# Two of the four normalisations in halves of 512 tokens, and the last FFN product behind the barrier

## What is computed

```
h = rms_norm(x, norm1_w); proj = h @ w_in                      # first
h2 = rms_norm(x, norm2_w); ... x + (silu(gate) * up) @ w_ffn_down   # second
h = rms_norm_2(x, g_pre); proj = h @ w_in_2                    # third
x = x + rms_norm_2(merged @ w_out, g_post)                     # fourth
```

## Time and profile before

| | |
|---|---|
| time, median of 3 runs | 3429.97 us (3427.22 to 3436.2) |
| the profiled execution | 3430.34 us |
| its span, first to last instruction | 3428.4 us |
| TensorE busy | 3283.3 us, 96% of the span |
| VectorE, ScalarE, GpSimd busy | 1479.0, 1012.7, 1315.8 us |
| mean granted TensorE clock | 0.983 |

### The profile page before, as it was taken

The page is one execution under the profiler, slowest core; times in us unless marked ns, Lnnn a source line. Parts: engine busy times, 40 slices in busy tenths (PEclk is TensorE's granted clock), DMA queues, the critical chain, the costliest instruction groups (busy, mean ns, idle before and its releaser), DMA issues. The chain is left out here.

```text
span 3428.4 us, 51094 instructions
## 1 busy us (share of the span) xinstructions
PE 3283.3 (96%) x20680; PEld 2707.5 (79%) x20680; DVE 1479.0 (43%) x2368; ACT 1012.7 (30%) x1728; POOL 1315.8 (38%) x1102
## 2 busy tenths in 40 slices
PE   6999999999898999999999999999899999999999
PEld 5888888777787887887788888888688877777877
DVE  4333333263656555457633333333382144444343
ACT  3444444432443434301211111111222044432221
POOL 4222222252424242335434333344434355554543
PEclk9999999999999999999899999999899999999999
DMA  2100000103112011214111111111331111111122
GB/s 105 36 32 32 31 32 32 38 22 112 37 32 56 20 49 28 87 54 156 51 57 49 43 49 49 49 49 49 120 87 47 48 46 42 52 46 46 58 86 80
DMA packets 104198, 188.06 MB, mean 55 GB/s; under 512 B 32328, under 2 KB 64712, under 8 KB 101328
## 3 DMA queue, kind: packets, MB, share of 16 engines
q1 hardware_dynamic: 91536, 179.19, 16.0%
q10 hardware_dynamic: 12480, 6.29, 0.6%
HBM read 158.33 MB, written 27.12 MB: 54 GB/s over the span
## 5 line engine op out<-in xcount | busy, mean ns | idle before, releaser
L303 PE MATMUL DP<-XH,WH 128*128 128x512 f32 x2592 | 832.6, 402 | 18.3 <-POOL WL L251 18.3
L249 POOL CAST WH<-WRAW 128x1024 fp32r<-128x1024 f32 (+2 forms) x258 | 269.2, 1043 | 1484.2 <-issue 900.5
L303 PE MATMUL DP<-XL,WH 128*128 128x512 f32 x2592 | 804.7, 392 | 0.0
L303 PE MATMUL DP<-XH,WL 128*128 128x512 f32 x2592 | 803.5, 391 | 0.0
L251 POOL TENSOR_TENSOR WL<-WRAW,WH 128x1024 fp32r<-128x1024 f32 (+2 forms) x258 | 588.5, 2281 | 20.8
L303 PEld LDWEIGHTS DP<-XH,WL 128*128 128x128 f32 x2592 | 488.7, 189 | 105.6
L303 PEld LDWEIGHTS DP<-XL,WH 128*128 128x128 f32 x2592 | 488.8, 189 | 105.0
L303 PEld LDWEIGHTS DP<-XH,WH 128*128 128x128 f32 x2592 | 467.6, 189 | 120.0 <-issue 24.3
L870 DVE SCALAR_TENSOR_TENSOR SS<-B,RQ,SBI 128x256 f32<-128x256 f32 (+2 forms) x192 | 74.3, 428 | 314.8 <-PE B L569 314.8
L379 DVE TENSOR_TENSOR XR<-XR,B 128x1024 f32<-128x1024 f32 x88 | 106.6, 1220 | 90.7 <-PE B L359 88.4
L2320 DVE SCALAR_TENSOR_TENSOR TG<-DP,COL,TG 128x1023 f32<-128x1023 f32 x44 | 56.4, 1283 | 199.8 <-ACT TG L2308 197.0
(11 more groups left out here) (480 smaller groups left out, 5176.3 us busy)
## 6 DMA issues: line engine op xcount, KB each, us to landing
WRAW<-in_w_up SPq DMA_DIRECT2D x44, 512.0 KB, 3.5
WRAW<-in_w_attn SPq DMA_DIRECT2D x36, 512.0 KB, 3.5
WRAW<-in_w_down SPq DMA_DIRECT2D x22, 512.0 KB, 3.5
XR<-in_x SPq DMA_DIRECT2D x8, 1024.0 KB, 8.0
WRAW<-in_w_dn SPq DMA_DIRECT2D x16, 512.0 KB, 3.8
aa_dram<-AA ACTq DMA_DIRECT2D x12, 512.0 KB, 3.3
YY<-yy_dram SPq DMA_DIRECT2D x12, 512.0 KB, 4.1
WRAW<-in_w_lrux SPq DMA_DIRECT2D x10, 512.0 KB, 3.4
```

Of the source, the lines that this page charges most:

```text
L249: pool.tensor_copy(WH[b.slot][:, 0:b.kt, :], WRAW[b.slot][:, 0:b.kt, :]).then_inc(w_hi, 1)
L303: mm = pe.matmul(DP[b.slot][:, half * H:half * H + H], w[b.slot][:, k, :], x[:, k, half * H:half * H + H], start=one, stop=end)
```

## The change

The tokens of c1 and c3 are cut in two halves; every step of the normalisation is done for tokens 0 to 511 and for 512 to 1023 by operations of half the size, in an order written out by hand. The product that follows does all eight tiles of the first half, then the second (`product2_halves`), with `norm_sum` and `norm_turn` of the second half at tiles 4 and 6 of the first. XR is loaded in halves, the second halves behind the first two weight blocks. VectorE's chain `prep_dve` is cut: its first nine operations (`prep_angle`) stay at the front, the other 21 stand behind the whole normalisation. Their two stores move from SyncE's queue to ScalarE's, and ScalarE waits for them (pr_sm) in front of attention. In c3, block ffn1 7 is computed by halves behind the barrier (`product4_halves`), which moves up to the end of block 6; s5x 1 gets a third buffer and both s5x splits stand right behind the barrier. The load of the root's table (`norm_warm`) is a step of its own. The second and fourth normalisations keep their form; counters are renumbered throughout, which is left out here with the rewritten helpers `norm_*`, which take a token range.

```diff
+        self.buf = 2 if (name, it, pos) == ("s5x", 0, 1) and isinstance(it, int) else pos % 2
...
-        WRAW = [at(f"WRAW{i}", 128 + 4 * i, [P, 8, P]) for i in range(2)]
-        WH = [at(f"WH{i}", 136 + 4 * i, [P, 8, P], F32R) for i in range(2)]
-        WL = [at(f"WL{i}", 144 + 4 * i, [P, 8, P], F32R) for i in range(2)]
+        WRAW = [at(f"WRAW{i}", 128 + 4 * i if i < 2 else 112, [P, 8, P]) for i in range(3)]
+        WH = [at(f"WH{i}", 136 + 4 * i if i < 2 else 116, [P, 8, P], F32R) for i in range(3)]
+        WL = [at(f"WL{i}", 144 + 4 * i if i < 2 else 120, [P, 8, P], F32R) for i in range(3)]
...
+            if b.before() is not None and b.buf < 2:
...
+        def product4_halves(pe, b, group, hi, lo, before):
+
+            pe.wait_ge(w_split, b.n + 1)
+            pe.wait_ge(psum_free[b.slot], b.loads - 1)
+            for half in range(2):
+                t = slice(half * H, half * H + H)
+                for o in range(4):
+                    pe.wait_ge(part_read, group * 4 + (o + 1 if half else o // 2 - 1))
+                    for k in range(2):
+                        before(half, o, k)
+                        for w, x, one, end in ((WH, hi, k == 0, False), (WH, lo, False, False), (WL, hi, False, k == 1)):
+                            mm = pe.matmul(BANK[4 + o], w[b.slot][:, 2 * o + k, :], x[:, k, t], start=one, stop=end)
+                    if half and o == 3:
+                        mm.then_inc(mm_done, 1)
+                    elif half or o:
+                        mm.then_inc(part_ready, 1)
+
+        def add_half(dve, b, group, half, o, dst, m0):
+
+            if half and o == 3:
+                dve.wait_ge(mm_done, b.n + 1)
+            else:
+                dve.wait_ge(part_ready, (group + half) * 3 + (o + 1 if half else max(o, 1)))
+            x = dst[:, m0 + o, half * H:half * H + H]
+            dve.tensor_tensor(x, x, BANK[4 + o], ALU.add).then_inc(part_read, 1)
+
...
+        def product2_halves(pe, blocks, hi, lo, cs, within=None):
+
+            for b in blocks:
+                pe.wait_ge(w_split, b.n + 1)
+                pe.wait_ge(psum_free[b.slot], b.loads - 1)
+            for half, c in enumerate(cs):
+                t = slice(half * H, half * H + H)
+                steps = [(b, k) for k in range(KD if half == 0 else 4) for b in blocks]
+                if half:
+                    steps += [(b, k) for b in blocks for k in range(4, KD)]
+                for b, k in steps:
+                    if b is blocks[0]:
+                        if half == 0 and within:
+                            within(k)
+                        pe.wait_ge(xh_ready, c.nt + k + 1)
+                        pe.wait_ge(nt_used, c.nt + k + 1)
+                    for w, x, one, end in ((WH, hi, k == 0, False), (WH, lo, False, False), (WL, hi, False, k == KD - 1)):
+                        mm = pe.matmul(DP[b.slot][:, t], w[b.buf][:, k, :], x[:, k, t], start=one, stop=end)
+                    if half and k == KD - 1:
+                        mm.then_inc(mm_done, 1)
 
         def norm_tiles(c):
...
+            def second_norm(k):
+                if k == 4:
+                    norm_sum(pe, c1[1])
+                if k == 6:
+                    norm_turn(pe, c1[1])
+
+            product2_halves(pe, [att_block(0, pos) for pos in range(2)], XH, XL, c1, second_norm)
...
+        def ffn_last_pe(pe):
+            def before(half, o, k):
+                if (half, o, k) == (1, 2, 1):
+                    norm_sum(pe, c3[0])
+
+            product4_halves(pe, Block("ffn1", 0, 7), FT - 1, FH2, FL2, before)
+            norm_turn(pe, c3[0])
+
+        def ffn_last_dve(dve):
+            a, b = c3
+            block, group = Block("ffn1", 0, 7), FT - 1
+
+            def add(half, o):
+                add_half(dve, block, group, half, o, XR, 4)
+
+            def scale(k):
+                scale_one(dve, a, k, XR, "gpre")
+
+            add4(dve, Block("ffn1", 0, 6), FT - 2, XR, (2,))
+            norm_add(dve, c3_all, 1)
+            add4(dve, Block("ffn1", 0, 6), FT - 2, XR, (3,))
+            norm_add(dve, c3_all, 2)
+            norm_add(dve, c3_all, 3)
+            add(0, 0)
+            for o in range(1, 4):
+                add(0, o)
+                norm_add(dve, a, 3 + o)
+            dve.sem_inc(psum_free[block.slot], 1)
+            norm_add(dve, a, 7)
+            add(1, 0)
+            norm_inverse(dve, a)
+            add(1, 1)
+            scale(0)
+            scale(1)
+            add(1, 2)
+            add(1, 3)
+            norm_add(dve, b, 4)
+            for k in range(2, 5):
+                scale(k)
+                norm_add(dve, b, k + 3)
+            scale(5)
+            scale(6)
+            norm_inverse(dve, b)
+            scale(7)
+            norm_scale(dve, b, XR, "gpre")
+
+        def ffn_last_act(act):
+            a, b = c3
+            act.wait_ge(fl_ready, FT)
+            for k in range(4):
+                act.wait_ge(part_read, (FT - 2) * 4 + k + 1)
+                norm_square(act, c3_all, k, XR[:, k, :])
+            norm_warm(act)
+            for k in range(4, KD):
+                act.wait_ge(part_read, (FT - 1) * 4 + k - 3)
+                norm_square(act, a, k, XR[:, k, a.tok])
+            norm_sqrt(act, a)
+
+            def square(k):
+                act.wait_ge(part_read, FT * 4 + k - 3)
+                norm_square(act, b, k, XR[:, k, b.tok])
+
+            hi_one(act, a, 0)
+            hi_one(act, a, 1)
+            square(4)
+            square(5)
+            hi_one(act, a, 2)
+            square(6)
+            hi_one(act, a, 3)
+            square(7)
+            for k in range(4, 7):
+                hi_one(act, a, k)
+            norm_sqrt(act, b)
+            hi_one(act, a, 7)
+            norm_hi(act, b)
 
...
-            sp.wait_ge(pr_sm, 1)
-            sp.dma_start(r8_dram, SM[:, 8, :]).then_inc(pr_out, 16)
-            sp.dma_start(sk_dram, SM[:, 13:27, :].rearrange("p r t -> p (r t)")).then_inc(pr_out, 16)
...
-        def prep_dve(dve):
+        def prep_angle(dve):
...
+        def prep_dve(dve):
...
-                    sp.dma_start(XR[:, 2 * i:2 * i + 2, :], a["x"][:, 2 * i:2 * i + 2, :]).then_inc(mx_in[i], 16)
+                    sp.dma_start(XR[:, 2 * i:2 * i + 2, 0:H], a["x"][:, 2 * i:2 * i + 2, 0:H]).then_inc(mx_in[i], 16)
...
+                for k, n, landed in ((0, 2, mx_out), (2, 2, ks_out), (4, 4, w1_out)):
+                    sp.dma_start(XR[:, k:k + n, H:T], a["x"][:, k:k + n, H:T]).then_inc(landed, 16)
...
-                split(pool, Block("s5x", 0, 0))
-                pool.wait_ge(sq_used, c3.acc + 7)
-                split(pool, Block("s5x", 0, 1))
...
+                def square1(i, k):
+                    act.wait_ge((mx_out, ks_out, w1_out, w1_out)[k // 2] if i else mx_in[k // 2], 16)
+                    norm_square(act, c1[i], k, XR[:, k, c1[i].tok])
+
                 for k in range(KD):
-                    act.wait_ge(mx_in[k // 2], 16)
-                    norm_square(act, c1, k, XR[:, k, :])
-                norm_sqrt(act, c1)
-                norm_hi(act, c1)
+                    square1(0, k)
+                norm_warm(act)
+                norm_sqrt(act, c1[0])
+                hi_one(act, c1[0], 0)
+                hi_one(act, c1[0], 1)
+                for k in range(5):
+                    square1(1, k)
+                for k in range(5, KD):
+                    hi_one(act, c1[0], k - 3)
+                    square1(1, k)
+                hi_one(act, c1[0], 5)
+                hi_one(act, c1[0], 6)
+                norm_sqrt(act, c1[1])
+                hi_one(act, c1[0], 7)
+                norm_hi(act, c1[1])
...
+                prep_angle(dve)
+                for k in range(1, KD):
+                    norm_add(dve, c1[0], k)
+                norm_inverse(dve, c1[0])
+                dve.wait_ge(con_in, 32)
+
+                def scale1(i, k):
+                    scale_one(dve, c1[i], k, XR, "norm1")
+
+                scale1(0, 0)
+                scale1(0, 1)
+                for k in range(1, 5):
+                    norm_add(dve, c1[1], k)
+                for k in range(5, KD):
+                    scale1(0, k - 3)
+                    norm_add(dve, c1[1], k)
+                scale1(0, 5)
+                scale1(0, 6)
+                norm_inverse(dve, c1[1])
+                for k in range(7, KD):
+                    scale1(0, k)
+                for k in range(KD):
+                    scale1(1, k)
                 prep_dve(dve)
-                for k in range(1, KD):
-                    norm_add(dve, c1, k)
...
+            sp.wait_ge(part_read, 4 * (FT + 1))
```

More of the change, by code:

```diff
@@ L394, in program, with __init__ @@
         class NormCount:
-            def __init__(self, i):
-                self.sq, self.ss, self.nt = KD * i, i, KD * i
-                self.acc, self.root = 7 * i, 2 * i
+            def __init__(self, sq, acc, nt, root, tokens=(0, KD), sums=None, spread=None, nt0=None):
```

(47 more changed lines are left out.)

116 lines of the change are left out of this document (59 added, 57 removed).

## The result

| | before | after |
|---|---|---|
| median | 3430.99 us (13 runs) | 3438.53 us (13 runs) |
| lowest to highest | 3418.51 to 3437.13 | 3432.12 to 3445.33 |
| profiled execution, its span | 3430.34, 3428.4 | 3443.1, 3441.0 |
| mean granted clock | 0.983 | 0.980 |

The ratio of the times is 1.0027, 95% interval 1.0018 to 1.0036: some 9 us slower (6 to 12). The forecast was 3431.5 (3414 to 3441).

What follows compares the result with a forecast made beforehand. TensorE, busy 96% of the span, was taken as the bound, so only its waits or slow work could pay. Start +6.0 and FFN end -4.7 gave +1.3 us on 3430.34: 3431.5 us predicted, range 3414 to 3441.

Steps and rivals of the forecast that it cites:

- First matmul at 24.8: Start: the first product's first matmul comes at 24.8 us, 12.5 us earlier than before.
- Adds held inside the product: First product: adds wait for GpSimd's subtractions, 3.3 us a tile for tiles 2 to 4; block 0 done at 57.5.
- The moved chain: Behind the first product: one small operation passes per GpSimd operation, pr_sm 10.5 us behind block 0, TensorE waits 7.3 us.
- one of the forecast's own signs of being wrong: Profile after: no gap of TensorE at j = 17, behind block 2's first tile, would show the forecast wrong.
- The clock behind the wait: Start, behind TensorE's wait: 14 matmuls at half speed cost 2.8 us, 2.0 of it outside the sums; start +6.0.
- FFN -4.7: End of the FFN: s5x starts at 2429.1, the next block at 2456.9 in place of 2461.63, 4.7 us gained.
- The rest of the program "shifts": Second normalisation and everything else: the same instructions, only shifted in time; no term in the sum.
- rival 3: Start and FFN end: TensorE's clock stays at 1.2 GHz through the bursts, +10 us on the sum, 3441.5; chance 0.13.
- 1 (chain slips through): Start: only the adds are held, not the small chain's operations, so the 7.3 us wait goes; 3422 us, chance 0.24.
- 2 (nothing held): Both places: neither adds nor chain are held by GpSimd; start -13, FFN -9.5, 3408 us; chance 0.13.
- 4 (nothing): Both places: gains and costs all under 1 us; its chance counted within the forecast's 0.50.

Runs made afterwards that it cites:

- e2: The changed kernel with the third normalisation taken back to whole tiles, so only the first is in halves; ratio 1.0049 to before.
- e4: The changed kernel with ScalarE's wait for the small chain and its two stores moved behind take_q(0) and take_k(0); ratio 1.0002 to before.
- e8: The kernel of e4, unchanged, profiled once more; one run, 3426.64 us.
- e10: The kernel of e4, unchanged, timed again; ratio 0.9993 to before.
- e7: The changed kernel, unchanged, profiled once more; one run, 3442.19 us.
- e6: The kernel before the change, unchanged, profiled once more; one run, 3427.89 us.
- e3: The changed kernel with the 21 small operations back in front of the adds and their stores back on SyncE; ratio 1.0008 to before.
- e9: The changed kernel with the first normalisation's running sums in PSUM, only the last add of each half writing SBUF; ratio 1.0011 to before.
- e5: The kernel of e4 with the first normalisation's running sums in PSUM as well; ratio 0.9967 to before.
- e1: The changed kernel with the first normalisation, x's loads, small chain and stores taken back, so only the third is in halves; ratio 0.9993 to before.
- e11: The kernel of e1 with the first normalisation's running sums, in whole tiles, in PSUM; ratio 0.9972 to before.

## Why the prediction was nearly right, and where its sum was not

**First matmul at 24.8.** Measured 22.49 in the first profile and 24.62 in the second, with add 7 ending at 14.84 and 16.83 (forecast 17.1). The working is that of the second; the first is the case in which the adds win the race against the weights. e2, e4, e8 and e10 (24.64 to 24.74) side with the second.

**Adds held inside the product.** Right: 3.21 us a tile (forecast 3.3), TensorE's gaps 2.03 and 1.60, sums of the second half at 36.85 behind adds ending at 36.80 (39.2 with a start 2.3 later). Behind the adds the working was 3 us short: from the first matmul to the end of block 0 it has 30.8 us (32.7 with the clock's 2), and it took 33.8 after and 34.0 in e7. I had TensorE set the pace of the second half, and GpSimd's subtractions did, 1.4 us each. That block 0 was done at 56.3, near the 57.5 taken, is luck of the early first matmul; in e7 it was 58.6.

**The moved chain.** Right in kind: 12.3 us in place of 4.5, one held per GpSimd operation, the stores on ScalarE ahead of ASQ, TensorE waiting. pr_sm came at 56.3 + 9.3 (forecast + 10.5). The place was wrong: TensorE stops 9.62 us at block 2's first matmul, which waits for `take_q` to free that block's PSUM slot, and not 7.3 us at j = 17 behind it, where there is no gap: one of the forecast's own signs of being wrong. The price came out the same by luck, because the forecast's later pr_sm made up for the eviction QA and three pairs of matmuls that it left out: block 2 starts at 68.76 in place of 64.49, +4.3 (forecast +4.0). In e7, the case that was worked out, it starts at 71.05: +6.6.

**The clock behind the wait: the mis-sized term.** Forecast 2.0, from 14 slow matmuls; measured 5.0 (the shift grows from 4.3 at 68.76 to 9.3 at 79.8). The sums, which I had taken out, slow down too: 3.41 for 1.84. With it the start is +9.3 in place of +6.0. Against e6, where before itself loses 3.1 behind its own wait, 1.9 of the 5.0 are left.

**FFN -4.7.** Right: -4.7 to -5.5 in every kernel that has it, idle 3.22 (3.2), s5x at 2428.8 (2429.1), next block 2457.7 (2456.9).

**The rest of the program "shifts".** Wrong, and missing from the sum: the same instructions took some 9 us more between 736 and 1566 us (in e7 5.8, +12.1 to +17.9), 5.2 of them beside a fall of the clock from 749 to 769. 3.8 of the rest lie behind 1000 us, where e7 has 0.6. From the terms read, +9.3 - 4.7 leaves +4.6; with those 5.2 it is +9.8, and the times say +9 (1.0027); with profiles of one kernel up to 5 us apart at their ends this agreement is no proof of the terms. The time lies in the stated range because its upper end leaves room for part of rival 3; the sum itself, +1.3, was some 8 us short. The step of about +5 appears in every kernel with halves at the start whose shift at 736 us was above -1 (after, e2, e3, e7, e8, with +3.6 in e9), and in e10 at -1.8; not in e4 (-1.3), e5 or the three without halves there (e1, e6, e11). That it hangs on when TensorE reaches that place is argued, not shown: e4 and e10 are one kernel. What makes the clock fall while TensorE is busy stays open, and no run was made that changes that place alone.

**Rivals.** 1 (chain slips through) falls by 12.3 us; its price was near e4, where nobody waits for the chain. 2 (nothing held) falls by 1.34 for 0.69; e5 and e9 show what it would take. 3 (clock) was half true: the lower clock cost 5 at the start and 5 near 750, and the time lies near its 3441.5, but half of that cost arose where this rival had put nothing. In the bursts, for which it was put, it did less: tiles 2 to 4 ran at 227 ns after, though in e7 the windows 22 to 37 and 37 to 47 us stood at 0.80 and 0.79; and at the FFN's end there was less of it, 3.4 us against 20.5 before, where TensorE stood nearly idle: the ten profiles with this part have 3.4 us there or none, the three without it 20.5 or more. 4 (nothing) falls.

## To carry to other kernels

When a step is moved behind other work, look first at what its consumer's queue holds behind the wait: here two stores, for whose data TensorE was not waiting, stood ahead of the eviction that frees its slot, and sending them later was worth some 12 us at the start. Before splitting a chain of VectorE adds to hide it, look whether they are held by GpSimd; a running sum in PSUM took that away by one edit, and whole tiles with it were as fast as halves. And a long wait of TensorE is priced with everything that runs behind it at half clock, its sums too.

## What the runs showed of the hardware that was not expected

- TensorE's clock fell to 1.2 GHz for 20 us (749 to 769 us, granted 0.50) with TensorE busy 10.00 of each 10 us ahead of and through the fall. What it did ahead of the fall had changed: 46 matmuls in each 10 us until 730, then 38, some of them on 8 partitions.
- The same wait of 2.32 us was followed by full speed in one profile of before, and by 6.8 us at the lower clock in the other (e6).
- What holds a VectorE add beside GpSimd's subtraction is its second SBUF input, not where it writes: 1.40 with two inputs in SBUF and the output in PSUM, 0.69 with one and the output in SBUF (e9).
- A transfer that landed 0.5 us earlier came with a first product 2.1 us later, as the order of two engines' operations turned over.
- At the very start the clock record and the durations disagree: after's window from 22 to 37 us shows 1.00 (the record has no entry before 28.4), while its first 12 matmuls came 427 ns apart. There the durations tell the level, and the last column of the table leaves this stretch out.
- After 9.6 us of TensorE idle, a granted clock of 0.50 for the next 11 us; after 3.2 us idle (2426.20 after) full speed at once, 0.39 to 0.40 a matmul.
